# Turn tables as sines under the heads' projection, and a Fourier stage on half its features and frequencies

## What is computed

```python
dt = jnp.exp(log_dt.astype(jnp.float32))[:, None]
mag = jnp.exp(lr * dt)
ab_re = mag * jnp.cos(li * dt)
ab_im = mag * jnp.sin(li * dt)
...
_, _, s_re, s_im = lax.associative_scan(_complex_affine_combine, (a_re, a_im, v_re, v_im), axis=1)
```

```python
fh = f.reshape(bn, L, FNET_HEADS, FNET_HEAD_DIM).astype(jnp.float32)   # 4 heads of 128
spec = jnp.fft.fft2(fh, axes=(1, 3), norm="ortho").real
return spec.astype(f.dtype).reshape(bn, L, FNET_WIDTH) @ w_f
```

## Time and profile before

| | us |
|---|---|
| median of 3 runs (3650.06 to 3652.96) | 3651.37 |
| the profiled execution | 3658.59 |
| its span, first to last instruction | 3656.8 |
| PE busy | 3337.6 (91%) |
| DVE busy | 2016.3 (55%) |
| ACT busy | 930.4 (25%) |
| POOL busy | 295.0 (8%) |
| mean granted clock of TensorE | 0.950 of 2.4 GHz |

### The profile page before, as it was taken

The page is one execution under the profiler, slowest core; times in us unless marked ns, Lnnn a source line. Parts: engine busy times, 40 slices in busy tenths (PEclk is TensorE's granted clock), DMA queues, the critical chain, the costliest instruction groups (busy, mean ns, idle before and its releaser), DMA issues. The chain is left out here.

```text
span 3656.8 us, 47803 instructions
## 1 busy us (share of the span) xinstructions
PE 3337.6 (91%) x20190; PEld 3051.6 (83%) x20190; DVE 2016.3 (55%) x2794; ACT 930.4 (25%) x1159; POOL 295.0 (8%) x327
## 2 busy tenths in 40 slices
PE   3999999999679699999999999899898968999787
PEld 3999999999667499999999999899898945555445
DVE  5565655565679245566366367544545536666236
ACT  3222232222314231121011011211323224444213
POOL 0000000000257000000000000000031001222000
PEclk9999999999789699999999999999999988999898
DMA  2221232222452344411311413211111320000221
GB/s 98 89 88 63 89 99 83 85 88 69 164 87 60 102 155 133 133 58 47 127 58 47 132 53 98 86 44 49 56 67 65 129 103 0 1 1 1 94 81 69
DMA packets 102167, 287.97 MB, mean 79 GB/s; under 512 B 13120, under 2 KB 31936, under 8 KB 101568
## 3 DMA queue, kind: packets, MB, share of 16 engines
q1 hardware_dynamic: 101952, 284.90, 24.1%
HBM read 220.88 MB, written 63.98 MB: 78 GB/s over the span
## 5 line engine op out<-in xcount | busy, mean ns | idle before, releaser
L491 PE MATMUL mixer_in_dense<-mix_z_high,mixer_in_whigh 128*128 128x348 f32 x1344 | 444.5, 331 | 11.3 <-POOL mixer_in_out L328 11.3
L491 PE MATMUL mixer_in_dense<-mix_z_high,mixer_in_wlow 128*128 128x348 f32 x1344 | 437.5, 326 | 0.0
L491 PE MATMUL mixer_in_dense<-mix_z_low,mixer_in_whigh 128*128 128x348 f32 x1344 | 436.6, 325 | 0.0
L1325 PE MATMUL flow_dense<-rst_norms_operand_b_high,flow_whigh 128*128 128x342 f32 x1248 | 399.2, 320 | 0.4 <-DVE flow_wlow L1417 0.4
L1325 PE MATMUL flow_dense<-irst_norms_operand_b_low,flow_whigh 128*128 128x342 f32 x1248 | 398.3, 319 | 0.0
L1325 PE MATMUL flow_dense<-rst_norms_operand_b_high,flow_wlow 128*128 128x342 f32 x1248 | 397.4, 318 | 0.0
L1883 PE MATMUL joint_dense<-rst_norms_operand_b_high,joint_whigh 128*128 128x342 f32 (+2 forms) x1056 | 344.5, 326 | 17.6 <-DVEq L2000 10.1
L1883 PE MATMUL joint_dense<-rst_norms_operand_b_high,joint_wlow 128*128 128x342 f32 (+2 forms) x1056 | 341.4, 323 | 0.0
L1883 PE MATMUL joint_dense<-irst_norms_operand_b_low,joint_whigh 128*128 128x342 f32 (+2 forms) x1056 | 340.3, 322 | 0.0
L1325 PE MATMUL flow_dense<-first_operand_a_high,flow_whigh 128*128 128x342 f32 (+1 forms) x912 | 291.4, 320 | 27.1 <-DVEq L1438 27.1
L1325 PE MATMUL flow_dense<-first_operand_a_low,flow_whigh 128*128 128x342 f32 (+1 forms) x912 | 291.8, 320 | 0.0
(11 more groups left out here) (515 smaller groups left out, 6327.7 us busy)
## 6 DMA issues: line engine op xcount, KB each, us to landing
mixer_in_wstage<-w_in SPq DMA_DIRECT2D x56, 512.0 KB, 4.5
mixer_in_mod_w<-w_mod SPq DMA_DIRECT2D x64, 384.0 KB, 3.5
first_norms_weights<-w_up SPq DMA_DIRECT2D x44, 512.0 KB, 3.3
flow_side<-h SPq DMA_DIRECT2D x24, 512.0 KB, 4.3
h<-flow_out SPq DMA_DIRECT2D x24, 512.0 KB, 2.9
first_norms_weights<-ab_w_in SPq DMA_DIRECT2D x20, 512.0 KB, 3.3
p<-mixer_in_out SPq DMA_DIRECT2D x16, 528.0 KB, 2.9
first_norms_weights<-w_down SPq DMA_DIRECT2D x16, 512.0 KB, 3.3
```

What stands on the lines that cost most here:

```text
L491: mm = pe.matmul(pd[s % 2][:, 0:W], a[n % 2][:, P * m:P * (m + 1)], z[x][:, m, W * b:W * (b + 1)], start=m == 0 and i == 0, stop=m == DT - ...
L1325: mm = pe.matmul(o, w[n % NW][:, P * k:P * (k + 1)], x[h][:, k, where], start=k == 0 and e == 0, stop=k == kt - 1 and e == 2)
```

## The change

**In heads_out** the loads come in another order: first weights, then lam_re, lam_im and log_dt, then yb through four buffers (only the 1026 columns that are used), then the second weights, the other parameters and a new table `steps` (0, 1, 2, ...), then the gates' inputs. The pieces get new places: those numbered -8 to -1 run behind the high or low half of yb tile s + 8, in both engines' order. PE has four banks instead of two. The turn tables 0 and 1 are no longer built on POOL: DVE reduces 8 times the angle to a fraction of a turn ("turns") and for each table takes steps x fraction, less the nearest whole number (three operations of 1056 elements); ACT then writes |fraction| (Abs), the sine and, from the absolute value, the cosine (two Sin). POOL only sets one constant. The outer product 0 becomes two copies on ACT, the skip diagonal goes to slot 21.

**In s5** ACT waits for four clears, spreads b 0 and 1, and only then waits for all six.

**The Fourier stage** keeps of the features the frequencies 0 to 63 as cosines and as sines and one middle column (129 columns), and of the tokens' frequencies 257 of each parity. Two heads share a 128-row operand. Even and odd parts are multiplied with the sum and the difference of fnet_w and its mirror image, and the outputs at k and -k are their sum and their difference, read forwards and backwards by DVE. All eight PSUM banks form a ring; SP loads all inputs without a wait.

```diff
-    W, NP, NQ = NM // 3, NPAIR, 8
+    W, NP, NQ, RING = NM // 3, NPAIR, 8, 4
+    BIG, TURN = 1.5 * 2.0 ** 23, 6.2831848
     NS = 3 * DT
     ca, pwt, b_re, b_im, skip_diag, rot, m8, w_re, w_im = keep
     at = {}
-    for s, name, k in ((1, "vectors", 0), (2, "angles", 0), (3, "base", 0), (4, "power", 2), (4, "power", 3), (5, "power", 4),
-                       (5, "power", 5), (6, "power", 6), (6, "power", 7), (7, "power", 8), (7, "rotation", 0),
-                       (8, "coefficients", 0), (9, "reverse", 0), (9, "scaled_b", 0), (10, "negate", 0), (10, "outer", 0),
-                       (12, "outer", 1), (13, "outer", 2), (15, "outer", 3), (16, "outer", 4), (18, "outer", 5),
-                       (19, "outer", 6), (21, "outer", 7), (22, "outer", 8), (NS, "skip", 0)):
+    for s, name, k in ((-8, "step", 0), (-7, "angles", 0), (-5, "base", 0), (-4, "power", 2), (-4, "power", 3),
+                       (-3, "power", 4), (-3, "power", 5), (-2, "power", 6), (-2, "power", 7), (-1, "power", 8),
+                       (0, "turns", 0), (1, "rotation", 0), (1, "reverse", 0), (2, "coefficients", 0), (2, "negate", 0),
+                       (3, "table", 0), (4, "scaled_b", 0), (5, "vectors", 0), (6, "table", 1), (7, "outer", 1),
+                       (9, "outer", 2), (11, "outer", 3), (12, "outer", 4), (14, "outer", 5), (16, "outer", 6),
+                       (17, "outer", 7), (19, "outer", 8), (20, "outer", 0), (21, "skip", 0)):
...
+                def load_yb(m):
+                    sp.dma_start(ring[m % 4][:, :], t["yb"][m][:, FIRST:FIRST + NM]).then_inc(yb_landed[m % 4], 16)
+
                 load(0)
-                for m in range(HH):
-                    if m >= 2:
-                        sp.wait_ge(x_low, m - 1)
-                    sp.dma_start(a[m % 2][:, :], t["yb"][m]).then_inc(yb_landed[m % 2], 16)
-                    if m == 1:
-                        load(1)
+                for buf, n in steps_of:
+                    sp.dma_start(buf[:], t[n]).then_inc(steps_in, 16)
+                for m in range(4):
+                    load_yb(m)
+                for m in range(4, HH):
+                    sp.wait_ge(x_low, m - 3)
+                    load_yb(m)
+                load(1)
+                for buf, n in loads:
+                    sp.dma_start(buf[:], t[n]).then_inc(params_in, 16)
                 load_side(0)
                 load_side(1)
-                for buf, n in loads:
-                    sp.dma_start(buf[:], t[n]).then_inc(params_in, 16)
...
+                    elif name == "table":
+                        act.wait_ge(wrapped, k + 1)
+                        if k == 0:
+                            act.wait_ge(quartered, 1)
+                        act.activation(w_re[k][:, :, :], angle[:, :, :], ACT.Abs).then_inc(folded, 1)
+                        act.activation(w_im[k][:, :, :], angle[:, :, :], ACT.Sin, scale=-TURN).then_inc(tabled, 1)
+                        act.wait_ge(folded, k + 1)
+                        act.activation(w_re[k][:, :, :], w_re[k][:, :, :], ACT.Sin, bias=quarter[:, 0:1],
+                                       scale=-TURN).then_inc(tabled, 1)
+                    elif name == "outer" and k == 0:
+                        act.wait_ge(params_in, 16 * len(loads))
+                        act.activation(ca[:, :, 0, 0, :], cr[:, :, :], ACT.Copy).then_inc(first_rows, 1)
+                        act.activation(ca[:, :, 1, 0, :], ci[:, :, :], ACT.Copy, scale=-1.0).then_inc(first_rows, 1)
...
+                    for name, k in at.get(m - HH, ()):
+                        piece(name, k)
...
-                    if s >= 2:
-                        pe.wait_ge(moved, s - 1)
+                    if s >= RING:
+                        pe.wait_ge(moved, s - RING + 1)
...
-                ch = Chain(pool, pstep)
-                pool.wait_ge(rotated, 1)
-                for n in range(2):
-                    turn_table(pool, ch, rot, w_re[n], w_im[n], pu, pv, n, NQ)
+                pool.memset(quarter[:, :], float(np.pi / 2)).then_inc(quartered, 1)
...
+                    elif name == "turns":
+                        ch.do(ts(kk[:, :], r[:, :], 8 / TURN, BIG, ALU.mult, ALU.add))
+                        ch.do(ts(kk[:, :], kk[:, :], BIG, None, ALU.subtract))
+                        ch.do(ts(turn[:, :], r[:, :], 8.0, None, ALU.mult))
+                        for part in (6.28125, 0.0019350051879882812, 3.019915981956752e-07):
+                            ch.do(stt(out=turn[:, :], in0=kk[:, :], scalar=-part, in1=turn[:, :], op0=ALU.mult,
+                                      op1=ALU.add))
+                        ch.do(ts(turn[:, :], turn[:, :], float(1 / (2 * np.pi)), None, ALU.mult))
+                    elif name == "table":
+                        if k == 0:
+                            dve.wait_ge(params_in, 16 * len(loads))
+                        else:
+                            dve.wait_ge(tabled, 2 * k)
+                        ch.do(tt(w_im[k][:, :, :], steps[:, :].unsqueeze(1).broadcast_to([P, NQ, NCH]),
+                                 turn[:, NQ * k:NQ * (k + 1)].unsqueeze(2).broadcast_to([P, NQ, NCH]), ALU.mult))
+                        ch.do(ts(angle[:, :, :], w_im[k][:, :, :], BIG, None, ALU.add))
+                        ch.do(stt(out=angle[:, :, :], in0=angle[:, :, :], scalar=BIG, in1=w_im[k][:, :, :],
+                                  op0=ALU.subtract, op1=ALU.subtract))
+                        dve.sem_inc(wrapped, 1)
...
-                act.wait_ge(zeroed, 6)
+                act.wait_ge(zeroed, 4)
                 spread_b(0)
                 spread_b(1)
+                act.wait_ge(zeroed, 6)
...
+    LT, HT, HF, HK = SEQ // P, SEQ // P // 2, P // 2, SEQ // 4 + 1
+    QF = P + 1
+    GROUPS = ((0, 3), (3, 6), (6, 8))
...
                 sp.dma_start(dd[:, :], t["dft_features"]).then_inc(const, 16)
-                sp.dma_start(w[:, :, :], t["fnet_w"]).then_inc(const, 16)
-                for h in range(2):
+                for h in range(4):
                     sp.dma_start(fin[h][:, :], z[h]).then_inc(landed[h], 16)
-                sp.dma_start(dl[:, :, :, :], t["dft_tokens"]).then_inc(tokens_in, 16)
-                for h in range(2, 4):
-                    sp.wait_ge(first, 4 * (h - 1))
-                    sp.dma_start(fin[h % 2][:, :], z[h]).then_inc(landed[h % 2], 16)
+                sp.dma_start(dl[:, :, :, :, :], t["dft_tokens"]).then_inc(tokens_in, 16)
+                for buf, n in ((wn, "fnet_w"), (wr, "fnet_w_mirrored"), (w_mid, "fnet_w_middle")):
+                    sp.dma_start(buf[:], t[n]).then_inc(w_in, 16)
                 for m in range(4):
-                    if m >= 2:
-                        sp.wait_ge(done, m - 1)
-                    sp.dma_start(fg[m % 2][:, :], z[4 + m]).then_inc(g_landed[m % 2], 16)
+                    sp.dma_start(fg[m][:, :], z[4 + m]).then_inc(gates_in, 16)
...
+                def features(h, i):
+                    o = take(("features", h, i))[0]
+                    for u, q in enumerate(range(*GROUPS[i])):
+                        mm = pe.matmul(o[:, QF * u:QF * (u + 1)], fin[h][:, P * q:P * q + P], dd[:, :], start=True, stop=True)
+                    mm.then_inc(full, 1)
+
+                def tokens(pair, part, b):
+                    o = take(("tokens", pair, part, b))[0]
+                    for q in range(HT):
+                        mm = pe.matmul(o[:, 0:HK], eo[b][:, pair, part, q, :], dl[:, part, q, b, :], start=q == 0,
+                                       stop=q == HT - 1)
+                    mm.then_inc(full, 1)
+
+                def middle(b):
+                    o = take(("middle", b))[0]
+                    for q in range(HT):
+                        mm = pe.matmul(o[0:4, 0:HK], eo_mid[b][:, q, :], dl[:, 0, q, b, :], start=q == 0, stop=q == HT - 1)
+                    mm.then_inc(full, 1)
+
+                def out(m, part):
+                    for b, o in enumerate(take(("out", m, part))):
+                        for pair in range(2):
+                            mm = pe.matmul(o[:, 0:HK], ws[part][:, pair, P * m:P * m + P], sp_[:, pair, part, b, :],
+                                           start=pair == 0, stop=part == 1 and pair == 1)
+                        if part == 0:
+                            mm = pe.matmul(o[:, 0:HK], w_mid[:, P * m:P * m + P], sp_mid[:, b, :], start=False, stop=True)
+                    mm.then_inc(full, 1)
...
+                pe.wait_ge(const, 16)
                 for h in range(4):
+                    pe.wait_ge(landed[h], 16)
+                    for i in range(3):
+                        features(h, i)
+                pe.wait_ge(tokens_in, 16)
+                for pair in range(2):
+                    pe.wait_ge(folded, 2 * pair + 2)
+                    for part in range(2):
+                        for b in range(2):
+                            tokens(pair, part, b)
+                pe.wait_ge(folded, 5)
```

(41 more changed lines are left out.)

422 lines of the change are left out of this document (228 added, 194 removed).

## The result

The changed kernel takes **3593.99 us** (median; 3590.92 to 3603.62) against 3652.16 of the kernel before beside it, 58.2 us less by the medians. The ratio of the two kernels is put at 0.9833, 95% interval 0.9822 to 0.9845 (the quotient of the medians is 0.9841). The forecast was 3591.5. The profiled execution spans 3601.8 us (3656.8 before), 55.0 less.

What follows compares the result with a forecast made beforehand. TensorE, busy 91% of the span, was taken as the bound: fewer columns or closed gaps shorten a stage. Savings of 53.2 (Fourier), 3.5 (s5) and 3.1 (heads_out), 59.8 us, off the median 3651.4 gave 3591.5 us; range 3575 to 3602.

Steps and rivals of the forecast that it cites:

- the largest term: Fourier stage: fewer matmul columns end it at 3477.6 instead of 3530.8, 53.2 us saved, all on the path.
- Fourier, features: Fourier stage: 64 records of 129 columns at 0.19 us each take 12.2 us, plus 1.5 for the clock.
- The clock's share: Fourier stage, start: PE's clock at 0.50 there costs 1.5 us.
- Fourier, output: Fourier stage: 40 output matmuls, 80 records at 0.217 us, take 17.3 us (before 27.7).
- rival C: Fourier stage: halving paid in part elsewhere (feature records, reversed read, late start, clock), 9.7 us, 3601 us; chance 0.14.
- s5: s5 stage: ACT's spread of b waits for the first four memsets only and starts earlier, 3.5 us saved.
- heads_out: Projection of the heads: last move at 1055.4 instead of 1058.5, 3.1 us saved.
- The wait for the gates: heads_out: DVE's move 3 waits for a gate queued on ACT behind the table, 6.8 us in all.
- PE's stalls: heads_out: PE idles 7.7 us ahead of tile 6 and 4.6 ahead of tile 9, each costing 2.2 of clock.
- Rival B: heads_out: the gates are not felt, 15.7 us more saved, kernel at 3576 us; chance 0.10.
- Rival D: heads_out: parameter chain delays the loads, table pieces take longer by a drain per switch, 5 us, 3596.5; chance 0.10.
- Rival E: heads_out: new stalls keep PE's clock at 0.50, kernel slower than before, 3675 us if all 22 tiles; chance 0.02.

## Why the prediction was right, point by point

The total was right, 58.2 us saved against 59.8, and so were the mechanisms. Inside the largest term two errors, 3.5 us too much and 3.4 too little, cancelled; that the Fourier stage came out at 53.2 to the tenth is luck.

- **Fourier, features: 13.7 us forecast, 10.15 measured.** The step that failed is the 0.19 us a record, taken from the earlier trace rows. At the full clock a record took 0.112 us: it did halve with its columns (0.217 with 257, 0.112 with 129), close to the 0.113 that I had worked out and set aside for the weight loads. The row was the wrong one, since its records alternate between 128 and 64 rows: 18 records of 0.113 and six changes of height of 0.20 are its 3.20 us. The clock's share was too low in turn: 1.5 us forecast, 3.0 measured (10.15 less 64 x 0.112), as the clock stayed at 0.50 for 6 us behind PE's start. That time varies: over the eleven profiles of this stage the clock rose 3.8 to 6 us behind the start, and the features took 9.1 to 10.2 us.
- **Fourier, output: 17.3 forecast, 20.7 measured.** The price of 0.217 a record holds, as the tiles with 128 rows show. Missing was the cost of 16 changes of height, 3.1 us in all (20.69 us against 17.57 without them).
- **The rest of it:** start 4.3 us behind the first load (4.6), tokens 14.0 (13.9), the middle row 3.6 (3.5), its wait 0.77 (0.7), tail 6.3 (6.0). Tiles came 5.1 us apart with PE busy and DVE waiting for ACT's copy between them, so rival C (reversed reads, DVE as the bound) didn't occur; the reversed subtract took 0.68 us, and weight loads didn't set the pitch of the features.
- **s5: 3.5 forecast, 3.0 by the means of three and ten profiles.** The start moved by the whole 3.5.
- **heads_out: 3.1 forecast, 4.2 in the profile, 4.6 by means.** The wait for the gates (6.8 forecast, 7.05), PE's stalls (7.7 and 4.6; 7.99 and 4.54), and their cause were right. Mis-sized were the last low half, 0.7 us earlier than said, and the clock behind a stall, on average 1.9 us and not 2.2. My sentence that PE has four banks and so needs no move was true and worth nothing in this kernel: with two banks the stage is as long.
- **Rival B's price** (the gates not felt, 3576) came out as a kernel of its own, at 3578. **Rival D:** by the Trainium skill (ScalarE: Activation LUTs, "What ACT_TABLE_LOAD costs") a switch would have cost 2.66 us. The trace disagrees: it shows a load of 1.28 and the next function 0.02 us behind it, and the kernel without switches 1.4 for each. By the same page ("Table sets") abs is in every set; the trace agrees, since the load of the sines stood behind Abs, at 968.23. **Rival E:** the clock came back both times; the third window behind the first stall shows 0.73.

## What to carry to other kernels

Before pricing a matmul from a row, take the distance between two starts and not the count in a window, and look at the rows of its weights and of its neighbours': 0.19 to 0.2 us went into each change between 128 and 4 or 64 rows, and padding with zeros or grouping by height takes that away. A piece of work put on an idle engine costs what waits behind it in that engine's queue: put the piece behind the step that others wait for. And when parts of a change are worth 3 us in 3600, compare the lengths of stages over several profiles, since one stage varies more by itself, and hold each time against its own runs of before.
